# Final norm of an encoder with mixture of experts: who squares, scales and finishes each of the four tiles

## The chip, the cores and the metric

The kernel runs on one core of a Trainium2 chip. The metric is the device time of one execution in microseconds. A core has a matrix engine (TensorE, PE in the profile), three engines for elementwise work (VectorE or DVE, ScalarE or ACT, GpSimd or POOL) and SyncE (SP), whose queue issues most transfers. Each engine runs its own instructions in order, and engines wait for each other through semaphores.

## The reference

One layer of a bidirectional encoder on 512 tokens with 1024 channels: RMSNorm, a mixer (neighbourhood attention and gated linear attention), RMSNorm, a mixture of 32 experts (each token takes two), and a final RMSNorm. Cut to the end, on which the change works:

```python
def rmsnorm(x, g):
    xf = x.astype(jnp.float32)
    y = xf * lax.rsqrt(jnp.mean(xf * xf, axis=-1, keepdims=True) + RMS_EPS)
    return (y * g.astype(jnp.float32)).astype(x.dtype)

# in reference():
        h = rmsnorm(x, norm_ffn_g[l])
        x = x + hierarchical_moe(h, ...)      # x is x2 in the kernel
    return rmsnorm(x, final_norm_g)           # x2 * 1/root * gain, float32
```

## The kernel before, in words

The 512 tokens are four tiles of 128 rows (`TT = 4`, numbered 0 to 3), one row on each partition, 1024 columns (`D`) in float32. For most of the kernel TensorE multiplies by the experts' weights while SyncE loads them. The order of everything is written out by hand, one program for each engine.

The end is a pipeline over the four tiles:

- SyncE reads the stored expert outputs of each tile into `got`. TensorE adds up the rest of a tile (residual and the last expert) in two banks of PSUM, one for each half of 512 columns, and signals `share_done`.
- VectorE, in `add_up(t)`, adds `got` and the bank into `x2[:, t]`, half by half; each half counts `x2_done` up by one. So `x2_done` is 2 after tile 0, 8 after tile 3. Tile 1 is the one that `MIXED` names: two VectorE operations ahead of all tiles prepare it.
- ScalarE squares the tile with a running sum (`ssq3`; in the profile an ACTIVATE and an ACTIVATION_READ_ACCUMULATOR) and takes the root (`root3`).
- VectorE, in `final_root(t)`, takes the reciprocal of the root (`rstd3`).
- GpSimd multiplies tiles 0 to 2 by the gain `gfb` into `x2g`, one instruction a tile.
- ScalarE scales `x2g` by `rstd3` into `res` for tiles 0 to 2 (the Identity of line 1637); each is issued behind the root of the next tile.
- VectorE, in `last_tile()`, finishes tile 3 itself: one SCALAR_TENSOR_TENSOR for each half computes `x2 * rstd3 * gfb` (line 2255).
- SyncE waits for each result in the order of the tiles and stores it: three transfers of 512 KB (line 765), then two of 256 KB (line 769). Then it waits until all have landed, and the program ends.

A branch for tokens that overflow an expert's slots (`general > limit`) stands in the program and is not taken in these runs.

Of the kernel before, what the change touches and what calls it, by code (L numbers as in the profile page):

```python
# [224 lines left out]
def mixer_and_moe(nc, x, x_T, rpb, w_in, w_g2, b_g, gla_g, g_mix, w_out, g_ffn_T, w_r, b_r, w_all, g_fin,  # L225
                  c_small, c_mask, c_scan, c_tok, out, limit=SLOTS):
    with ExitStack() as ctx:
# [87 lines left out]
        def take(n):  # L315
            v = small[:, pos[0]:pos[0] + n]
            pos[0] += n
            return v
# [11 lines left out]
        ssq3, root3, rstd3 = take(TT), take(TT), take(TT)  # L330
        comb = take(2 * TT).rearrange("p (t k) -> p t k", k=2)
        most = take(1).bitcast(I32)
        eps = take(1)
        assert pos[0] <= 768

# [247 lines left out]
        def _(sp):  # L583
# [176 lines left out]
                    sp.dma_start(flat(down_unit(LAST)), down_d(e)).then_inc(a_w, 16)  # L760


            for t in range(TT - 1):
                sp.wait_ge(res_act, t + 1)
                sp.dma_start(out_d[t], res[:, t]).then_inc(out_stored, 16)
            for half in range(2):
                cols = slice(half * 512, (half + 1) * 512)
                sp.wait_ge(res_done, half + 1)
                sp.dma_start(out_d[TT - 1][:, cols], res[:, TT - 1, cols]).then_inc(out_stored, 16)
            sp.wait_ge(out_stored, 16 * (TT + 1))  # L770
            sp.wait_ge(page_cleared, 16)
            for t in range(TT):
# [635 lines left out]
        def _(act):  # L1408
# [217 lines left out]
                        nc.scalar.copy(g_hidT.rearrange("p a b -> p (a b)"), pbank[3][:]).then_inc(a_copied, 1)  # L1626

            nc.scalar.activation(oroot[:, 0, 0:1], oss[:, 0, 0:1], ACT.Sqrt)
            for t in range(TT):
                act.wait_ge(x2_done, 2 * (t + 1))  # L1630
                nc.scalar.activation(junk3[:, t], x2[:, t], ACT.Square, accum_out=ssq3[:, t:t + 1]).then_inc(sumsq_done, 1)
                act.wait_ge(sumsq_done, 3 * TT + t + 1)
                nc.scalar.activation(root3[:, t:t + 1], ssq3[:, t:t + 1], ACT.Sqrt, scale=1.0 / D, bias=eps).then_inc(root_done, 1)
                if t >= 1:
                    act.wait_ge(rstd_done, 2 * TT + t)
                    act.wait_ge(x2g_done, t)
                    nc.scalar.activation(res[:, t - 1], x2g[:, t - 1], ACT.Identity, scale=rstd3[:, t - 1:t]).then_inc(res_act, 1)


        @block.vector  # L1640
        def _(dve):
# [602 lines left out]
            def final_root(t):  # L2244
                dve.wait_ge(root_done, 2 * TT + t + 1)
                nc.vector.reciprocal(rstd3[:, t:t + 1], root3[:, t:t + 1]).then_inc(rstd_done, 1)

            def last_tile():
                t = TT - 1
                dve.wait_ge(x2_done, 2 * TT)  # L2250
                final_root(t)
                dve.wait_ge(rstd_done, 3 * TT)
                for half in range(2):
                    cols = slice(half * 512, (half + 1) * 512)
                    nc.vector.scalar_tensor_tensor(res[:, t, cols], x2[:, t, cols], rstd3[:, t:t + 1], gfb[:, cols], ALU.mult,
                                                   ALU.mult).then_inc(res_done, 1)

            dve.wait_ge(gf_in, 16)
            dve.wait_ge(most_done, 1)
# [1 line left out]
            with dve.If(general > limit):  # L2261
# [29 lines left out]
                dve.wait_ge(x2_done, 2 * TT)  # L2291
                nc.vector.memset(g_col, 0.0).then_inc(mix_step, 2)
                dve.wait_ge(mix_step, 2)
                for t in range(TT - 1):
                    final_root(t)
                last_tile()
            with dve.If(general < limit + 1):

                def add_up(t):
                    dve.wait_ge(pages_in[t], 32)  # L2300
                    for half in range(2):
                        cols = slice(half * 512, (half + 1) * 512)
                        dve.wait_ge(share_done, 2 * t + half + 1)
                        rest_of_it = pbank[SHARE_BANK[2 * t + half]][:]
                        if t == MIXED:
                            tt(x2[:, t, cols], got[0][:, t, cols], rest_of_it, ALU.add).then_inc(x2_done, 1)
                        else:
                            nc.vector.scalar_tensor_tensor(x2[:, t, cols], got[0][:, t, cols], comb_by[:, t, 0:1], rest_of_it,
                                                           ALU.mult, ALU.add).then_inc(x2_done, 1)

                dve.wait_ge(pages_in[MIXED], 32)
                nc.vector.tensor_scalar(got[1][:, MIXED], got[1][:, MIXED], comb_by[:, MIXED, 1:2], None,
                                        ALU.mult).then_inc(mix_step, 1)
                dve.wait_ge(mix_step, 1)
                nc.vector.scalar_tensor_tensor(got[0][:, MIXED], got[0][:, MIXED], comb_by[:, MIXED, 0:1], got[1][:, MIXED],
                                               ALU.mult, ALU.add).then_inc(mix_step, 1)
                add_up(0)
                dve.wait_ge(mix_step, 2)
                add_up(1)
                final_root(0)  # L2320
                add_up(2)
                final_root(1)
                add_up(3)
                final_root(2)
                last_tile()


        @block.gpsimd
        def _(pool):
# [33 lines left out]
                nc.gpsimd.indirect_dma_start(y_tok, bass.IndirectOffsetOnAxis(ap=tab_u[:, e:e + 1], axis=0), y_sb[e % RING], None,  # L2363
                                             bounds_check=last_row, oob_is_err=False).then_inc(y_stored[e % RING], 16)
            pool.wait_ge(gf_in, 16)
            for t in range(TT - 1):
                pool.wait_ge(x2_done, 2 * (t + 1))
                nc.gpsimd.tensor_tensor(x2g[:, t], x2[:, t], gfb, ALU.mult).then_inc(x2g_done, 1)


def constants():
# [73 lines left out]
```

## Time and profile before

| what | value |
|---|---|
| time, median of 3 runs | 736.91 us (736.15 to 736.98) |
| profiled execution, its own time | 737.39 us |
| span of its instructions | 735.6 us |
| PE busy | 718.7 us (98%) |
| DVE busy | 271.4 us (37%) |
| ACT busy | 146.6 us (20%) |
| POOL busy | 76.3 us (10%) |
| share of PE in the chain that ended last | 90% |
| mean DMA rate over the span | 327 GB/s |

The profiled execution lies 0.48 us over the median; its span leaves 1.8 us outside the first and the last instruction. TensorE is busy for nearly all of the span, but not in the last 8 us of it, and that is where the changed lines run. Shares over the whole span say nothing of that stretch, so it has to be read row by row.

### The profile page before, as it was taken

How to read it: one execution, taken by the hardware profiler on the slowest of the kernel's cores; microseconds unless marked ns; L12 is line 12 of the kernel's file. 1: busy time of each engine (PE TensorE's matmuls, PEld its weight loads, DVE VectorE, ACT ScalarE, POOL GpSimd, SP SyncE). 2: the span in 40 equal slices, each digit the busy share in tenths (PEclk: the TensorE clock that was granted, in tenths of full speed). 3: DMA queues.
4: the chain of work that ended last, by engine and by line, in shares of the span. 5: the costliest groups of instructions: out<-in, count | busy, mean ns of one | idle time of the engine just before them, and what ended most of it. 6: DMA issues, size and time to landing. Idle time of an engine off the chain costs nothing.

```text
span 735.6 us, 11813 instructions
## 1 busy us (share of the span) xinstructions
PE 718.7 (98%) x5112; PEld 411.6 (56%) x5117; DVE 271.4 (37%) x552; ACT 146.6 (20%) x315; POOL 76.3 (10%) x79
## 2 busy tenths in 40 slices
PE   9999999999999999999999999999999999998995
PEld 5488888888776664545544544544445445444431
DVE  2884463757987783111111111111111201201205
ACT  2652230134553550000000000000000000000014
POOL 0000049100000210010000010010010010000003
PEclk9999999999999999999999999999999999999998
DMA  9832332224934799999999999999999999999985
GB/s 326 265 114 93 142 112 73 99 67 158 412 118 174 269 355 380 425 430 424 397 421 429 439 429 437 432 419 438 429 419 429 434 421 428 427 424 428 423 344 210
DMA packets 31877, 240.79 MB, mean 327 GB/s; under 512 B 5606, under 2 KB 7014, under 8 KB 21456
## 3 DMA queue, kind: packets, MB, share of 16 engines
q1 hardware_dynamic: 29200, 235.94, 78.3%
q0 software_dynamic: 2480, 4.06, 1.5%
q8 instruction: 42, 0.69, 0.4%
q14 instruction: 11, 0.09, 0.0%
q10 hardware_dynamic: 144, 0.00, 0.0%
HBM read 231.74 MB, written 12.32 MB: 332 GB/s over the span
## 4 chain that ended last, share of the span: by engine, by line
PE 90%; DMA 7%; ACT 1%; DVE 1%; issue 0%; another core or an unknown queue 0%; DVEq 0%
PE bank L1272 27%; PE bank L785 17%; PE bank L1292 14%; PE bank L1213 9%; DMA arena<-in_w_all 7%; PE bank L829 4%; PE bank L1050 4%; PE bank L1106 3%; PE bank L1226 2%; PE bank L1281 1%; PE bank L1002 1%; PE bank L1088 1%; PE bank L1069 1%; PE bank L1147 1%; PE bank L1325 1%; PE bank L979 1%
## 5 line engine op out<-in xcount | busy, mean ns | idle before, releaser
L1272 PE MATMUL bank<-arena 128*64 128x512 f32 x1024 | 226.9, 593 | 3.9 <-DMA arena<-in_w_all 3.8
L1272 PEld LDWEIGHTS bank<-arena 128*64 128x64 f32 x1024 | 73.6, 137 | 148.8 <-issue 148.4
L785 PE MATMUL bank<-arena 128*128 128x256 f32 x560 | 123.2, 380 | 0.0
L1292 PE MATMUL bank<-arena 128*64 128x512 f32 x512 | 116.9, 598 | 0.2
L785 PEld LDWEIGHTS bank<-arena 128*128 128x128 f32 x560 | 105.7, 190 | 15.5 <-issue 1.5
L1643 DVE TENSOR_TENSOR arena<-arena 128x512 f32<-128x512 f32 (+12 forms) x129 | 96.0, 784 | 9.3 <-ACT arena L1411 6.1
L2188 DVE SCALAR_TENSOR_TENSOR arena<-bank,arena 128x256 f32<-128x256 f32 x32 | 15.5, 484 | 217.2 <-ACT arena L1597 217.1
L1213 PEld LDWEIGHTS bank<-arena 128*128 128x128 bf16 x1344 | 75.3, 98 | 22.2 <-issue 21.9
L1597 ACT ACTIVATE arena<-bank,arena 128x256 f32<-128x256 f32 x32 | 15.2, 475 | 339.9 <-PE bank L1272 334.1
L1213 PE MATMUL bank<-arena 128*128 128x128 bf16 (+1 forms) x1344 | 81.6, 217 | 0.0
L2363 POOL DMA_INDIRECT y_tok<-arena x31 | 30.3, 976 | 406.2 <-DVE arena L2195 378.4
L1292 PEld LDWEIGHTS bank<-arena 128*64 128x64 f32 x512 | 34.1, 136 | 58.4 <-issue 54.8
L2195 DVE COPY arena<-bank 128x512 f32<-128x512 f32 x32 | 22.1, 692 | 117.8 <-PE bank L1292 117.8
L1643 DVE TENSOR_TENSOR arena<-bank,arena 128x512 f32<-128x512 f32 (+1 forms) x49 | 32.6, 667 | 61.8 <-PE bank L1213 23.5
L829 PE MATMUL bank<-arena 128*128 128x512 f32 x64 | 28.8, 606 | 0.4 <-DVE arena L1650 0.4
L1411 ACT ACTIVATE arena<-bank 128x512 f32<-128x512 f32 x20 | 11.9, 596 | 81.7 <-PE bank L785 81.7
L1050 PE MATMUL bank<-arena 128*128 128x256 f32 x112 | 27.8, 391 | 0.0
L1106 PE MATMUL bank<-arena 128*128 128x512 f32 x56 | 25.3, 597 | 0.0
L1602 ACT COPY arena<-bank 128x256 f32<-128x256 f32 x32 | 11.9, 373 | 62.1 <-PE bank L1281 62.1
L1643 DVE TENSOR_TENSOR arena<-arena,bank 128x512 f32<-128x512 f32 (+1 forms) x31 | 20.6, 669 | 7.0 <-PE bank L1106 4.5
L1050 PEld LDWEIGHTS bank<-arena 128*128 128x128 f32 x112 | 20.1, 189 | 5.2 <-issue 2.7
L2356 POOL TENSOR_TENSOR arena<-arena 128x512 bf16<-128x512 f32 x8 | 8.3, 1042 | 127.6 <-DVE arena L1643 127.6
(179 smaller groups left out, 482.6 us busy)
## 6 DMA issues: line engine op xcount, KB each, us to landing
arena<-in_w_all SPq DMA_DIRECT2D x47, 2048.0 KB, 31.3
arena<-in_w_all SPq DMA_DIRECT2D x7, 6144.0 KB, 28.2
arena<-in_w_all SPq DMA_DIRECT2D x8, 4096.0 KB, 30.0
arena<-in_w_all SPq DMA_DIRECT2D x18, 1024.0 KB, 10.6
arena<-in_w_in SPq DMA_DIRECT2D x5, 2048.0 KB, 8.5
arena<-in_w_all SPq DMA_DIRECT2D x11, 512.0 KB, 5.2
arena<-in_x SPq DMA_DIRECT2D x8, 512.0 KB, 6.5
arena<-in_w_out SPq DMA_DIRECT2D x4, 1024.0 KB, 14.2
```

The source lines that it names most:

```text
L785: mm = pe.matmul(pbank[product_bank(g, p)][:, tile * 256:(tile + 1) * 256], lhs, rhs, start=(p in (1, 2, 5) and tile == 0 and k == 0), sto ...
L829: mm = pe.matmul(pbank[2 + t][:], gx[:, k, t * P:(t + 1) * P], w_buf[0][:, k], start=(k == 0), stop=(k == KC - 1))
L1050: mm = pe.matmul(pbank[share_bank(h, p)][:, tile * 256:(tile + 1) * 256], a[:, k, tile * P:(tile + 1) * P], w[:, k], start=(p in (1, 2, 5) ...
L1106: mm = pe.matmul(pbank[near_bank(m, p)][:], a[:, k], w[:, k], start=(p in (1, 2, 5) and k == 0), stop=(k == 1), skip_group_check=p in (6, ...
L1213: mm = pe.matmul(pbank[ROW_BANK[half]][:, k * P:k * P + n], h2_part[t][i][:, KC // 2 * half + k], pick[:, t, 0:n], start=(t == 0 and k == ...
L1272: mm = pe.matmul(both, xT[:, k, rows], gate_and_up(e, k)[:, :, cols], start=(k == 0), stop=(k == KC - 1))
L1292: mm = pe.matmul(pbank[down_bank(e)][64 * half:64 * half + 64, :], hidT[:, kc % 2, kc // 2], down_unit(e)[:, kc, half * 512:(half + 1) * 512],
L1597: nc.scalar.activation(hid[e % RING], pbank[GATE_BANK][:, 0:256], ACT.Silu, scale=rstd_slot[:, e:e + 1]).then_inc(sil_done, 1)
L1643: return nc.vector.tensor_tensor(out_, a, b, op)
L2188: nc.vector.scalar_tensor_tensor(hid[e % RING], pbank[GATE_BANK][:, 256:512], rstd_slot[:, e:e + 1], hid[e % RING], ALU.mult, ALU.mult).th ...
L2195: nc.vector.tensor_copy(y_sb[e % RING], pbank[down_bank(e)][:]).then_inc(y_evicted, 1)
L2363: nc.gpsimd.indirect_dma_start(y_tok, bass.IndirectOffsetOnAxis(ap=tab_u[:, e:e + 1], axis=0), y_sb[e % RING], None, bounds_check=last_row ...
```

## The change: the last RMSNorm is dealt out anew

Tile by tile:

- Tile 0: GpSimd multiplies only the first half by the gain, ScalarE scales that half; VectorE computes the second half in one SCALAR_TENSOR_TENSOR (`gained(0, 1)`), placed between the reciprocal of tile 0 and `add_up(2)`.
- Tile 1: GpSimd multiplies by the gain as before, and then scales the tile by `rstd3` too (a `tensor_scalar` on 1024 columns). ScalarE has no part in it but square and root. VectorE's reciprocal of tile 1 moves between the two halves of `add_up(2)`.
- Tile 2: VectorE computes both halves (`gained(2, 0)`, `gained(2, 1)`). GpSimd and ScalarE's Identity drop out.
- Tile 3: ScalarE squares the two halves in two instructions, each as soon as its half of `x2` is there. VectorE turns the first sum into a bias (`ms_half = ssq / D + eps`, one instruction on one column), and ScalarE's root adds it to the second sum. GpSimd multiplies the second half by the gain and ScalarE scales it, VectorE computes the first half.
- SyncE waits for the new semaphores and stores in the same order and the same sizes.

```diff
--- before.py
+++ after.py
@@ -330,6 +330,7 @@
         ssq3, root3, rstd3 = take(TT), take(TT), take(TT)
         comb = take(2 * TT).rearrange("p (t k) -> p t k", k=2)
         most = take(1).bitcast(I32)
+        ssq_half, ms_half = ssq2[:, 0, 0:1], ssq2[:, 0, 1:2]
         eps = take(1)
         assert pos[0] <= 768
 
@@ -760,13 +761,17 @@
                     sp.dma_start(flat(down_unit(LAST)), down_d(e)).then_inc(a_w, 16)
 
 
-            for t in range(TT - 1):
-                sp.wait_ge(res_act, t + 1)
-                sp.dma_start(out_d[t], res[:, t]).then_inc(out_stored, 16)
-            for half in range(2):
-                cols = slice(half * 512, (half + 1) * 512)
-                sp.wait_ge(res_done, half + 1)
-                sp.dma_start(out_d[TT - 1][:, cols], res[:, TT - 1, cols]).then_inc(out_stored, 16)
+            sp.wait_ge(res_act, 1)
+            sp.wait_ge(res_done, 1)
+            sp.dma_start(out_d[0], res[:, 0]).then_inc(out_stored, 16)
+            sp.wait_ge(x2g_done, 3)
+            sp.dma_start(out_d[1], res[:, 1]).then_inc(out_stored, 16)
+            sp.wait_ge(res_done, 3)
+            sp.dma_start(out_d[2], res[:, 2]).then_inc(out_stored, 16)
+            sp.wait_ge(res_done, 4)
+            sp.dma_start(out_d[TT - 1][:, 0:512], res[:, TT - 1, 0:512]).then_inc(out_stored, 16)
+            sp.wait_ge(res_act, 2)
+            sp.dma_start(out_d[TT - 1][:, 512:D], res[:, TT - 1, 512:D]).then_inc(out_stored, 16)
             sp.wait_ge(out_stored, 16 * (TT + 1))
             sp.wait_ge(page_cleared, 16)
             for t in range(TT):
@@ -1626,15 +1631,26 @@
                         nc.scalar.copy(g_hidT.rearrange("p a b -> p (a b)"), pbank[3][:]).then_inc(a_copied, 1)
 
             nc.scalar.activation(oroot[:, 0, 0:1], oss[:, 0, 0:1], ACT.Sqrt)
-            for t in range(TT):
+            for t in range(TT - 1):
                 act.wait_ge(x2_done, 2 * (t + 1))
                 nc.scalar.activation(junk3[:, t], x2[:, t], ACT.Square, accum_out=ssq3[:, t:t + 1]).then_inc(sumsq_done, 1)
                 act.wait_ge(sumsq_done, 3 * TT + t + 1)
                 nc.scalar.activation(root3[:, t:t + 1], ssq3[:, t:t + 1], ACT.Sqrt, scale=1.0 / D, bias=eps).then_inc(root_done, 1)
-                if t >= 1:
-                    act.wait_ge(rstd_done, 2 * TT + t)
-                    act.wait_ge(x2g_done, t)
-                    nc.scalar.activation(res[:, t - 1], x2g[:, t - 1], ACT.Identity, scale=rstd3[:, t - 1:t]).then_inc(res_act, 1)
+                if t == 1:
+                    act.wait_ge(rstd_done, 2 * TT + 1)
+                    act.wait_ge(x2g_done, 1)
+                    nc.scalar.activation(res[:, 0, 0:512], x2g[:, 0, 0:512], ACT.Identity, scale=rstd3[:, 0:1]).then_inc(res_act, 1)
+            t = TT - 1
+            act.wait_ge(x2_done, 2 * TT - 1)
+            nc.scalar.activation(junk3[:, t, 0:512], x2[:, t, 0:512], ACT.Square, accum_out=ssq3[:, t:]).then_inc(sumsq_done, 1)
+            act.wait_ge(x2_done, 2 * TT)
+            nc.scalar.activation(junk3[:, t, 512:D], x2[:, t, 512:D], ACT.Square, accum_out=ssq_half).then_inc(sumsq_done, 1)
+            act.wait_ge(sumsq_done, 4 * TT + 1)
+            act.wait_ge(mix_step, 3)
+            nc.scalar.activation(root3[:, t:], ssq_half, ACT.Sqrt, scale=1.0 / D, bias=ms_half).then_inc(root_done, 1)
+            act.wait_ge(rstd_done, 3 * TT)
+            act.wait_ge(x2g_done, 4)
+            nc.scalar.activation(res[:, t, 512:D], x2g[:, t, 512:D], ACT.Identity, scale=rstd3[:, t:]).then_inc(res_act, 1)
 
 
         @block.vector
@@ -2245,15 +2261,28 @@
                 dve.wait_ge(root_done, 2 * TT + t + 1)
                 nc.vector.reciprocal(rstd3[:, t:t + 1], root3[:, t:t + 1]).then_inc(rstd_done, 1)
 
-            def last_tile():
-                t = TT - 1
+            def gained(t, half):
+                cols = slice(half * 512, (half + 1) * 512)
+                nc.vector.scalar_tensor_tensor(res[:, t, cols], x2[:, t, cols], rstd3[:, t:t + 1], gfb[:, cols], ALU.mult,
+                                               ALU.mult).then_inc(res_done, 1)
+
+            def first_tile():
+                final_root(0)
+                dve.wait_ge(rstd_done, 2 * TT + 1)
+                gained(0, 1)
+
+            def last_tiles():
+
+                dve.wait_ge(sumsq_done, 4 * TT)
+                nc.vector.tensor_scalar(ms_half, ssq3[:, TT - 1:], 1.0 / D, EPS, ALU.mult, ALU.add).then_inc(mix_step, 1)
+                final_root(2)
                 dve.wait_ge(x2_done, 2 * TT)
-                final_root(t)
+                dve.wait_ge(rstd_done, 3 * TT - 1)
+                gained(2, 0)
+                gained(2, 1)
+                final_root(3)
                 dve.wait_ge(rstd_done, 3 * TT)
-                for half in range(2):
-                    cols = slice(half * 512, (half + 1) * 512)
-                    nc.vector.scalar_tensor_tensor(res[:, t, cols], x2[:, t, cols], rstd3[:, t:t + 1], gfb[:, cols], ALU.mult,
-                                                   ALU.mult).then_inc(res_done, 1)
+                gained(3, 0)
 
             dve.wait_ge(gf_in, 16)
             dve.wait_ge(most_done, 1)
@@ -2291,14 +2320,16 @@
...
             with dve.If(general < limit + 1):
 
                 def add_up(t):
                     dve.wait_ge(pages_in[t], 32)
                     for half in range(2):
+                        if (t, half) == (2, 1):
+                            final_root(1)
                         cols = slice(half * 512, (half + 1) * 512)
                         dve.wait_ge(share_done, 2 * t + half + 1)
                         rest_of_it = pbank[SHARE_BANK[2 * t + half]][:]
@@ -2317,12 +2348,10 @@
                 add_up(0)
                 dve.wait_ge(mix_step, 2)
                 add_up(1)
-                final_root(0)
+                first_tile()
                 add_up(2)
-                final_root(1)
                 add_up(3)
-                final_root(2)
-                last_tile()
+                last_tiles()
 
 
         @block.gpsimd
@@ -2363,9 +2392,15 @@
                 nc.gpsimd.indirect_dma_start(y_tok, bass.IndirectOffsetOnAxis(ap=tab_u[:, e:e + 1], axis=0), y_sb[e % RING], None,
                                              bounds_check=last_row, oob_is_err=False).then_inc(y_stored[e % RING], 16)
             pool.wait_ge(gf_in, 16)
-            for t in range(TT - 1):
-                pool.wait_ge(x2_done, 2 * (t + 1))
-                nc.gpsimd.tensor_tensor(x2g[:, t], x2[:, t], gfb, ALU.mult).then_inc(x2g_done, 1)
+            pool.wait_ge(x2_done, 2)
+            nc.gpsimd.tensor_tensor(x2g[:, 0, 0:512], x2[:, 0, 0:512], gfb[:, 0:512], ALU.mult).then_inc(x2g_done, 1)
+            pool.wait_ge(x2_done, 4)
+            nc.gpsimd.tensor_tensor(x2g[:, 1], x2[:, 1], gfb, ALU.mult).then_inc(x2g_done, 1)
+            pool.wait_ge(x2g_done, 2)
+            pool.wait_ge(rstd_done, 2 * TT + 2)
+            nc.gpsimd.tensor_scalar(res[:, 1], x2g[:, 1], rstd3[:, 1:2], None, ALU.mult).then_inc(x2g_done, 1)
+            pool.wait_ge(x2_done, 2 * TT)
+            nc.gpsimd.tensor_tensor(x2g[:, TT - 1, 512:D], x2[:, TT - 1, 512:D], gfb[:, 512:D], ALU.mult).then_inc(x2g_done, 1)
 
 
 def constants():
```

What stands in the engines' programs, as rows of line, operation, output and input, and semaphores waited for (`arena` is SBUF, `bank` PSUM). VectorE behind the last half of `add_up(1)`, before: the reciprocals of tiles 0, 1 and 2 stand between whole tiles.

```order
L1643 TENSOR_TENSOR arena<-arena,bank 128x512 [waits share_done]
L2246 RECIPROCAL arena<-arena 128x1 [waits root_done]
L2308 SCALAR_TENSOR_TENSOR arena<-arena,bank 128x512 [waits share_done,pages_in2]
L2308 SCALAR_TENSOR_TENSOR arena<-arena,bank 128x512 [waits share_done]
L2246 RECIPROCAL arena<-arena 128x1 [waits root_done]
L2308 SCALAR_TENSOR_TENSOR arena<-arena,bank 128x512 [waits share_done,pages_in3]
L2308 SCALAR_TENSOR_TENSOR arena<-arena,bank 128x512 [waits share_done]
```

The same place of the changed kernel (line 2266 is `gained`, 2262 the reciprocal, 2339 `add_up`):

```order
L1659 TENSOR_TENSOR arena<-arena,bank 128x512 [waits share_done]
L2262 RECIPROCAL arena<-arena 128x1 [waits root_done]
L2266 SCALAR_TENSOR_TENSOR arena<-arena 128x512 [waits rstd_done]
L2339 SCALAR_TENSOR_TENSOR arena<-arena,bank 128x512 [waits share_done,pages_in2]
L2262 RECIPROCAL arena<-arena 128x1 [waits root_done]
L2339 SCALAR_TENSOR_TENSOR arena<-arena,bank 128x512 [waits share_done]
L2339 SCALAR_TENSOR_TENSOR arena<-arena,bank 128x512 [waits share_done,pages_in3]
L2339 SCALAR_TENSOR_TENSOR arena<-arena,bank 128x512 [waits share_done]
```

An operation with both inputs in `arena` now stands ahead of `add_up(2)`; those of `add_up` have one input in `arena` and one in a bank. Behind them, at the end of VectorE's program, the changed kernel has these rows, where the one before had two reciprocals and two SCALAR_TENSOR_TENSOR:

```order
L2277 TENSOR_SCALAR arena<-arena 128x1 [waits sumsq_done]
L2262 RECIPROCAL arena<-arena 128x1 [waits root_done]
L2266 SCALAR_TENSOR_TENSOR arena<-arena 128x512 [waits rstd_done,x2_done]
L2266 SCALAR_TENSOR_TENSOR arena<-arena 128x512
L2262 RECIPROCAL arena<-arena 128x1 [waits root_done]
L2266 SCALAR_TENSOR_TENSOR arena<-arena 128x512 [waits rstd_done]
```

The reciprocal of tile 2 and both halves of tile 2 now stand behind the operation on tile 3's first sum. GpSimd's program ended in three multiplications of 1024 columns; in the changed kernel it ends so (line 2401 is the scaling of tile 1):

```order
L2392 DMA y_tok<-arena 2048x512 [waits y_evicted] x30
L2396 TENSOR_TENSOR arena<-arena 128x512 [waits x2_done,gf_in]
L2398 TENSOR_TENSOR arena<-arena 128x1024 [waits x2_done]
L2401 TENSOR_SCALAR arena<-arena 128x1024 [waits rstd_done,x2g_done]
L2403 TENSOR_TENSOR arena<-arena 128x512 [waits x2_done]
```

## Rows read from the trace of the kernel before

**Rows 1.** The page: the chain that ended last, by engine.

```profile
PE 90%; DMA 7%; ACT 1%; DVE 1%; issue 0%; another core or an unknown queue 0%; DVEq 0%
```

**Rows 2.** The chain that ended last, in order of time: start, us, what.

```profile
727.48 1.13 ACT arena L1637
728.61 1.05 ACT arena L1631 x2
...
730.08 0.17 DVE arena L2246
...
730.28 0.75 DVE arena L2255
```

**Rows 3.** Timeline of VectorE, the end: start, us, operation, count, idle before.

```profile
721.96 1.28 DVE L1643 TENSOR_TENSOR arena<-arena,bank 128x512 f32<-128x512 f32 x2
723.59 0.17 DVE L2246 RECIPROCAL arena<-arena 128x1 f32<-128x1 f32 x1 [0.35 <-ACT arena L1633]
724.65 1.41 DVE L2308 SCALAR_TENSOR_TENSOR arena<-arena,bank 128x512 f32<-128x512 f32 x2 [0.90 <-PE bank L1334]
725.97 0.16 DVE L2246 RECIPROCAL arena<-arena 128x1 f32<-128x1 f32 x1
726.57 1.54 DVE L2308 SCALAR_TENSOR_TENSOR arena<-arena,bank 128x512 f32<-128x512 f32 x2 [0.44 <-PE bank L1325]
```

**Rows 4.** Timeline of ScalarE, the end.

```profile
723.04 0.19 ACT L1631 ACTIVATION_READ_ACCUMULATOR arena<-arena 128x1 f32 x1
723.26 0.30 ACT L1633 ACTIVATE arena<-arena 128x1 f32<-128x1 f32 x1
723.46 1.04 ACT L1631 ACTIVATE arena<-arena 128x1024 f32<-128x1024 f32 x1
...
729.88 1.14 ACT L1637 ACTIVATE arena<-arena 128x1024 f32<-128x1024 f32 x1
```

**Rows 5.** Timelines of GpSimd and SyncE, the end; line 769 by itself.

```profile
722.20 7.02 POOL L2368 TENSOR_TENSOR arena<-arena 128x1024 f32<-128x1024 f32 x3 [18.23 <-DVE arena L2308]
...
731.04 0.33 SPq L765 DMA_DIRECT2D out<-arena  x1
...
731.42 0.43 SPq L769 DMA_DIRECT2D out<-arena  x1
...
L769 SPq DMA_DIRECT2D out<-arena x2: 431/610/789, 731.4 to 731.9; - x2
...
DMA to landing us min/median/max: 3.2/3.2/3.3
```

**Rows 6.** Busy time by stretches of 0.4 us; last: clock, DMA share, GB/s.

```profile
731.80:732.20 0.40, 0.00 (x0) 0.00 (x0) 0.00 (x0) 0.00 (x0) 0.00 (x0) 0.50 0.85 348
...
734.60:735.00 0.40, 0.00 (x0) 0.00 (x0) 0.00 (x0) 0.00 (x0) 0.00 (x0) 0.50 0.05 15
```

**Rows 7.** Timelines of GpSimd and VectorE where they overlapped; line 2340 by itself.

```profile
107.96 1.22 DVE L1643 TENSOR_TENSOR arena<-arena 128x1024 f32<-128x1024 f32 x1
...
L2340 POOL COPY arena<-arena x8: 1056/1078/2141, 102.9 to 111.1; 128x512 f32<-128x512 f32 x8
...
261.94 1.10 DVE L1643 TENSOR_TENSOR arena<-arena 128x128 bf16<-128x128 f32 x1
261.85 1.04 POOL L2356 TENSOR_TENSOR arena<-arena 128x512 bf16<-128x512 f32 x1 [0.96 <-DVE arena L1643]
...
267.24 0.28 DVE L2042 SCALAR_TENSOR_TENSOR arena<-arena 128x1 f32<-128x1 f32 x1 [0.45 <-ACT arena L1532]
266.46 1.04 POOL L2356 TENSOR_TENSOR arena<-arena 128x512 bf16<-128x512 f32 x1 [3.57 <-DVE arena L1643]
```

**Rows 8.** Timeline of ScalarE at 243.5 us: a square of 512 columns.

```profile
243.50 0.63 ACT L1532 ACTIVATE arena<-arena 128x512 f32<-128x512 f32 x1
244.03 0.19 ACT L1532 ACTIVATION_READ_ACCUMULATOR arena<-arena 128x1 f32 x1
244.13 0.60 ACT L1553 COPY arena<-arena 128x512 bf16<-128x512 bf16 x1
```

More of the change, by code:

```diff
@@ L2293, in _ @@
                 dve.wait_ge(mix_step, 2)
-                for t in range(TT - 1):
-                    final_root(t)
-                last_tile()
+                first_tile()
+                final_root(1)
+                last_tiles()
             with dve.If(general < limit + 1):
@@ L2301, in add_up @@
                     for half in range(2):
+                        if (t, half) == (2, 1):
+                            final_root(1)
                         cols = slice(half * 512, (half + 1) * 512)
@@ L2319, in _ @@
                 add_up(1)
-                final_root(0)
+                first_tile()
                 add_up(2)
-                final_root(1)
                 add_up(3)
-                final_root(2)
-                last_tile()
+                last_tiles()
         @block.gpsimd
@@ L2365, in _ @@
             pool.wait_ge(gf_in, 16)
-            for t in range(TT - 1):
-                pool.wait_ge(x2_done, 2 * (t + 1))
-                nc.gpsimd.tensor_tensor(x2g[:, t], x2[:, t], gfb, ALU.mult).then_inc(x2g_done, 1)
+            pool.wait_ge(x2_done, 2)
[7 more added lines that the diff above has]
+            nc.gpsimd.tensor_tensor(x2g[:, TT - 1, 512:D], x2[:, TT - 1, 512:D], gfb[:, 512:D], ALU.mult).then_inc(x2g_done, 1)
 def constants():
```

## The prediction, made before the change was run

> **What bounds the kernel now.** I read the page first: the chain that ended last is 90% TensorE [rows 1], but the changed lines all run behind 722 us, and VectorE waits for TensorE there for the last time at 726.57 [rows 3]. So the question is only what sets the end of the last 14 us. The chain in order of time gives it: ScalarE scales tile 1 at 727.48, squares tile 3 at 728.61, VectorE takes the reciprocal at 730.08 and computes the first half of tile 3 at 730.28 [rows 2]. ScalarE is the tight engine here: VectorE has finished tile 3's `x2` at 726.57 + 1.54 = 728.11 [rows 3], and the square starts only when ScalarE is through with tile 1, so tile 3 loses 0.5 us there.
>
> Behind the last computation lies the output. SyncE issues tile 2 at 731.04 (released by the Identity that ends at 729.88 + 1.14 = 731.02 [rows 4]), then the halves of tile 3 at 731.42 and 731.9 [rows 5]. These three hold 512 + 256 + 256 KB. The DMA engines move at full rate from 731.8, and nothing is left from 734.6 on [rows 6]: 1 MB in one burst of 2.8 us, which starts 0.8 us behind the issue of tile 2. The last half was issued at 731.9 and alone would need some 0.7 us of transfer behind the same 0.8 us, so it would be moved by 733.4; it ended at 734.6 because it queued. **The end of the kernel therefore follows the issue of tile 2, not that of tile 3**, as long as the halves of tile 3 are issued less than about 1.2 us later than now relative to it. All sums below are for this moment, 731.04.
>
> **What VectorE and GpSimd do to each other.** The change gives VectorE operations with both inputs in SBUF (`gained` reads `x2` and `gfb`) while GpSimd works. In the stage as it is no such pair meets: `add_up` has one input in a bank, and line 2255 runs when GpSimd is done (722.20 + 7.02 = 729.22 [rows 5]). Elsewhere it does. A VectorE operation of 128 columns that began at 261.94, just behind a GpSimd one (261.85 + 1.04 = 262.89), took 1.10 us, nearly as long as the 1.22 us of one with 1024 columns, and ended at 263.04. A SCALAR_TENSOR_TENSOR of one column began at 267.24 and took 0.28 us, until 267.52, where a GpSimd operation ended at 267.50; a reciprocal of one column takes 0.17 [rows 3]. The other way about, VectorE's operation at 107.96 took its plain 1.22 us, and of GpSimd's eight copies around it one took 2.14 us against a median of 1.08 [rows 7]. So the later of the two is held until the earlier is done, and a held VectorE operation ends at GpSimd's end plus its streaming time: 0.15 us for 128 columns, so about 0.55 for 512 (an estimate from the last two figures of rows 3 and 7: 0.75 us for a whole operation less the 0.15 to 0.2 that one column takes). A price of nothing for this meeting is the other bound.
>
> The Trainium skill says the same in the page "SBUF — State Buffer" (section Who interferes with whom): the second to issue fully blocks until the first is done. It speaks against this change, and the trace agrees with it at 261.94 (1.10 us for 128 columns). By the rule the sum is the +0.6 us below, without it the −1.0 us.
>
> **The change, part by part, with the hold.**
> 1. `gained(0, 1)`. The reciprocal of tile 0 is done at 723.76 [rows 3]; the operation would run from 723.8 to 724.55 and fit ahead of `add_up(2)`, which waits for TensorE until 724.65. But GpSimd's half of tile 0 takes about 1.19 us (7.02 / 3 = 2.34 for 1024 columns [rows 5], half of it and a little), 722.20 to 723.39, and tile 1's `x2` is there at 721.96 + 1.28 = 723.24. So GpSimd starts tile 1 at 723.40 and reads until 725.75. `gained(0, 1)` is held and ends at 725.75 + 0.55 = 726.30 instead of 724.55.
> 2. Queued behind it on VectorE: `add_up(2)`, the reciprocal of tile 1, `add_up(3)`. TensorE's shares are all there by 726.57 plus one half, so they go through back to back at a pitch of 0.66 (1.41 for two of 0.75) and 0.08 for the reciprocal: the first half from 726.21, reciprocal until 727.04, second half until 727.70 (before: 726.06), tile 3 until 728.36 and 729.03 (before: 728.11). Tile 2's `x2` is 1.6 us late, tile 3's 0.9 us.
> 3. ScalarE. Of three Identities of 1.14 us there remain a half of tile 0 and a half of tile 3. That frees it, so it waits for VectorE now. Square of tile 2 from 727.73, its its sum read 0.96 later (a square lasts 1.06, and the read begins 0.10 before its end [rows 8]), root 0.22 behind that at 728.91 until 729.21 (as 723.04 to 723.26 [rows 4]). The first half of tile 3 is squared 0.20 later, 729.11 (as 723.26 to 723.46), sum read at +0.53, done 729.83; the second half starts 0.10 behind that read's start [rows 8], 729.74, its sum is read at 730.27, root 730.49 to 730.79. Before, this root ended at 730.0: the halves do not pay back the 0.9 us.
> 4. The new wait. VectorE's `ms_half` needs the first sum, 729.83, and runs 729.87 to 730.02 (as a reciprocal). The reciprocal of tile 2 and both `gained(2, ...)` stand behind it, though tile 2's root was there at 729.21. Reciprocal until 730.11, then `gained(2, 0)` at 730.15.
> 5. GpSimd. The scaling of tile 1 waits for the reciprocal of 727.04 and starts at 727.08. No row shows a `tensor_scalar` on GpSimd. From below, I take half of the nearest row's rate, 1.05, since any value under 2.05 gives one result; by the nearest row, GpSimd's copies of 512 columns at 1.06 each, 1024 take 2.1; from above, the two-input 2.37. I take 2.1, the copy being the nearest in kind: until 729.2. Then tile 3's half, 729.2 to 730.4. `gained(2, 0)` meets it: 730.40 + 0.55 = 730.95 instead of 730.90. This hold costs 0.05 us, and 0.3 with 2.37; with anything under 2.05 nothing.
> 6. Tile 2's second half ends at 731.61, and SyncE issues tile 2 at 731.63 against 731.04: **+0.6 us**. Tile 3: reciprocal until 731.68, `gained(3, 0)` until 732.46, ScalarE's half (0.71: 0.63 for a square of that size plus the 0.08 between 1.14 and 1.06) until 732.4; issues at 732.49 and 732.93. That is 0.86 and 1.30 us behind tile 2's; before, 0.38 and 0.86. The burst from 732.4 lasts 2.8 us, the last half is ready for it at 733.7, so it still queues. Tiles 0 and 1 are issued at 726.3 and 729.2 and have left the DMA engines before 732.4.
>
> The GPSIMD page of the Trainium skill ("GPSIMD Engine Reference", section Performance versus the Vector engine) has one-input bodies at 1.03 cycles per element; no run here shows it for this operation. By it the scaling would take about 1 us, an estimate from that page, and the sum would be +0.55.
>
> **Sum.** Removed: 1.14 us twice from ScalarE ahead of tile 3. Added: a hold of 1.75 us on VectorE of which 1.6 reaches tile 2. Net at the issue of tile 2: +0.6 us. Against the profiled execution: span 735.6 to 736.2, time 737.39 to 738.0. The median of the runs shown lies 0.48 us lower, so 736.91 + 0.6 = 737.5 us.
>
> **The rivals.**
> - *No hold* (a SCALAR_TENSOR_TENSOR of this size gets through, or VectorE is there first). For it: margin between 723.40 and 723.80 is only 0.4 us. Against it: rows 7. Then `add_up(2)` ends at 726.19, square of tile 2 at 726.22, root until 727.70; tile 3's first half squared 727.60, second 728.23, root until 729.28; first sum 728.32, `gained(2, ...)` 728.64 to 730.05, issue of tile 2 at 730.07: −1.0 us, tile 3 at 730.93 and 731.35. Time 735.9.
> - *The end follows tile 3's issue instead.* If the last half needs its 3.2 us to land from 732.93, against 731.9 before [rows 5], the price is +1.0: 737.9.
> - *GpSimd's scaling is slow*, the case on the other side. Its place is between 727.08 and the last GpSimd half, and every us beyond 2.05 goes through `gained(2, 0)` to the issue of tile 2: the loss is its duration less 1.54. It becomes measurable from 3.0 us on; at 4.2, twice the copy's price, the loss is 2.7 us and the time 739.6. For it: the operation takes a scale from memory for each partition, which no GpSimd row has. Against it: the GpSimd rows here lie at 2.0 (1.04 for 512 columns [rows 7]) to 2.3 ns a column, and 3.0 would be needed.
> - *It doesn't do what it says*: the Identity of tile 1 left ScalarE for nothing if `x2` is late anyway; that is part 3 of the forecast.
>
> **How the numbers follow.** Hold and end by tile 2: 0.60, time 737.5, own range 737.2 to 737.8. End by tile 3: 0.10. No hold: 0.20. Slow scaling: 0.10. A measurement of this kernel tells a change from none at about 0.2%, 1.5 us. Neither +0.6, +1.0 nor −1.0 reaches that; what can is the slow scaling (0.10, and a little for two prices together) and the no-hold case with scatter in its favour (runs spread 0.8 us). Faster 0.06, same 0.82, slower 0.12. The range takes in no hold and the end by tile 3 with some scatter: 736.0 to 738.3.
>
> **What would show it.** Right: one SCALAR_TENSOR_TENSOR of 512 columns of about 2.5 us starting near 723.8 on VectorE; TensorE no longer the releaser of `add_up(2)`; the square of tile 2 near 727.7; a GpSimd `tensor_scalar` near 2.1 us; tile 2 issued near 731.6. Wrong: that operation at 0.75 us, the square of tile 2 at 726.2, tile 2 issued at 730.1; or a scaling over 3 us. The weakest steps are the streaming time of a held operation, the unseen `tensor_scalar`, and that the burst begins 0.8 us behind tile 2's issue.

## The result, and the profile after

The changed kernel is slower: the ratio of its time to that of the kernel before is 1.0026, 95% interval 1.0014 to 1.0038, which is 1.9 us (1.0 to 2.8). The medians over 22 runs each are 737.99 us and 735.89 us. The span of the profiled execution is 734.5 us, shorter than before. That tells nothing of the change: in this trace the last stage begins 2.45 us earlier (the first `add_up` operation starts at 718.19, against 720.64 before). In every trace here the stage is compared from that operation on; I call the time from there to the end of the span **the stretch**. Before it is 735.6 − 720.64 = 14.96 us, after it is 734.5 − 718.19 = 16.31 us: 1.35 us more. Two rows of VectorE's timeline before are needed for this section, the first `add_up` operations and the two of tile 3:

```profile
720.64 1.40 DVE L2308 SCALAR_TENSOR_TENSOR arena<-arena,bank 128x512 f32<-128x512 f32 x2
...
730.28 1.41 DVE L2255 SCALAR_TENSOR_TENSOR arena<-arena 128x512 f32<-128x512 f32 x2
```

The changed kernel's timeline, VectorE and then GpSimd (start, us, operation, count, idle before); rows of before are [rows 3] and [rows 5]:

```profile
718.19 1.40 DVE L2339 SCALAR_TENSOR_TENSOR arena<-arena,bank 128x512 f32<-128x512 f32 x2
...
721.33 2.56 DVE L2266 SCALAR_TENSOR_TENSOR arena<-arena 128x512 f32<-128x512 f32 x1
723.81 0.73 DVE L2339 SCALAR_TENSOR_TENSOR arena<-arena,bank 128x512 f32<-128x512 f32 x1
...
724.54 2.04 DVE L2339 SCALAR_TENSOR_TENSOR arena<-arena,bank 128x512 f32<-128x512 f32 x3
727.42 0.15 DVE L2277 TENSOR_SCALAR arena<-arena 128x1 f32<-128x1 f32 x1 [0.84 <-ACT arena L1645]
...
727.75 2.35 DVE L2266 SCALAR_TENSOR_TENSOR arena<-arena 128x512 f32<-128x512 f32 x2
```

```profile
719.75 1.27 POOL L2396 TENSOR_TENSOR arena<-arena 128x512 f32<-128x512 f32 x1 [18.27 <-DVE arena L2339]
720.98 2.35 POOL L2398 TENSOR_TENSOR arena<-arena 128x1024 f32<-128x1024 f32 x1
724.80 2.85 POOL L2401 TENSOR_SCALAR arena<-arena 128x1024 f32<-128x1024 f32 x1 [1.47 <-DVE arena L2262]
727.63 1.25 POOL L2403 TENSOR_TENSOR arena<-arena 128x512 f32<-128x512 f32 x1
```

Put the two lists side by side. VectorE's `gained(0, 1)` starts at 721.33, 0.35 us after GpSimd's multiplication of tile 1 has started. It lasts 2.56 us and ends at 723.89, 0.56 us behind that multiplication's end (723.33). The pair for tile 2 starts at 727.75, 0.12 us after the start of GpSimd's last operation, and takes 2.35 us, where line 2255 took 1.41 for two before (0.75 for one [rows 2]). `add_up`, with one input in a bank, keeps its pitch under GpSimd's scaling (2.04 for three), as it did under GpSimd's multiplications before (1.41 for two [rows 3, 5]).

ScalarE and SyncE of the changed kernel:

```profile
725.30 1.06 ACT L1636 ACTIVATE arena<-arena 128x1024 f32<-128x1024 f32 x1 [2.22 <-DVE arena L2339]
...
728.03 0.29 ACT L1650 ACTIVATE arena<-arena 128x1 f32<-128x1 f32 x1
730.20 0.72 ACT L1653 ACTIVATE arena<-arena 128x512 f32<-128x512 f32 x1 [1.88 <-DVE arena L2262]
```

```profile
730.12 0.33 SPq L770 DMA_DIRECT2D out<-arena  x1
730.98 0.33 SPq L772 DMA_DIRECT2D out<-arena  x1
731.36 0.45 SPq L774 DMA_DIRECT2D out<-arena  x1
```

ScalarE waits 2.22 us for tile 2 and 1.88 us for the reciprocal of tile 3, while before it had no gap over 0.12 us between 722.08 and 731.02. Tile 2 is issued at 730.12, 11.93 us behind the first `add_up` operation; before it was 731.04 − 720.64 = 10.40 [rows 5]. That is 1.53 us later, and the stretch is 1.35 us longer. The busy time by stretches (TensorE, its weight loads, VectorE, ScalarE, GpSimd; the last three are clock, DMA share, GB/s) shows the burst of 1 MB once more:

```profile
730.40:730.80 0.40, 0.00 (x0) 0.00 (x0) 0.40 (x1) 0.40 (x1) 0.00 (x0) 0.50 0.00 0
730.80:731.20 0.40, 0.00 (x0) 0.00 (x0) 0.16 (x1) 0.12 (x1) 0.00 (x0) 0.50 0.66 266
...
733.60:734.00 0.40, 0.00 (x0) 0.00 (x0) 0.00 (x0) 0.00 (x0) 0.00 (x0) 0.50 0.11 36
```

It begins some 0.8 us behind tile 2's issue and lasts 2.7 to 2.8 us, as in [rows 6].

### The profile page after: what moved, and what is told of

Same layout as the page of the kernel before. It is cut to its first block, busy times and chain, and to the rows that moved or that the text cites. A ratio compares the mean times of both kernels' runs of the same rounds, so it can differ in the third digit from the quotient of the medians.

```text
span 734.5 us, 11820 instructions
## 1 busy us (share of the span) xinstructions
PE 717.8 (98%) x5112; PEld 411.2 (56%) x5117; DVE 275.7 (38%) x555; ACT 144.7 (20%) x316; POOL 77.0 (10%) x80
## 4 chain that ended last, share of the span: by engine, by line
PE 85%; DMA 10%; ACT 2%; DVE 2%; issue 1%; SPq 1%; DVEq 0%; POOLq 0%
PE bank L1277 26%; PE bank L790 17%; PE bank L1297 14%; PE bank L1218 9%; DMA arena<-in_w_all 7%; PE bank L1055 4%; PE bank L1111 3%; PE bank L834 2%; PE bank L1231 2%; DMA arena<-in_x 1%; PE bank L1007 1%; PE bank L1286 1%; PE bank L1093 1%; DMA arena<-y_tok 1%; PE bank L1074 1%; DMA y_tok<-arena 1%
```

## The experiments

The theory: VectorE's operations with two SBUF inputs are held by GpSimd's two-input operations, and what this makes late is tile 2. The rivals: these operations are slow by themselves; the loss is GpSimd's slow scaling alone; the end follows tile 3. The stretch comes from one trace of one execution each; two traces of the same kernel differ by up to 0.3 us (the last section of experiments). The timed ratios, with intervals of about ±0.15% (1.1 us), carry less.

| kernel | `gained(0, 1)`, us | square of tile 2 starts at | tile 2 issued at | stretch | ratio to before (95%) |
|---|---|---|---|---|---|
| before | none | 5.45 | 10.40 | 14.96; again 14.71 | 1 |
| changed | 2.56 | 7.11 | 11.93 | 16.31; again 16.34 | 1.0026 (1.0014 to 1.0038) |
| 1 GpSimd waits | 0.75 | 5.50 | 9.76 | 15.04 | 1.0003 (0.9986 to 1.0020) |
| 2 VectorE ends tile 3 | 2.55 | 7.10 | 10.99 | 15.37 | 1.0002 (0.9988 to 1.0016) |
| 3 gain in PSUM | 0.75 | 5.89 | 9.75 | 14.38 | 0.9999 (0.9983 to 1.0014) |
| 4 ScalarE scales tile 1 | 2.55 | 7.52 | 11.39 | 15.76 | 1.0007 (0.9995 to 1.0019) |
| 5 = 1 and 2 | 0.75 | 5.50 | 9.77 | 15.10 | 1.0001 (0.9988 to 1.0015) |
| 6 tile 2 ahead of the sum | 2.55 | 7.10 | 11.33 | 15.69 | 1.0028 (1.0012 to 1.0044) |
| 7 no overlap | 0.75 | 5.45 | 9.45 | 14.78; again 13.94 | 0.9992 (0.9979 to 1.0004); 1.0005 (0.9988 to 1.0021) |
| 8 before, half of tile 0 alone | 2.54 | 7.03 | 11.98 | 16.37 | 1.0031 (1.0019 to 1.0042) |

Positions count from the start of the first `add_up` operation of the same trace.

### 1. GpSimd waits for VectorE's half of tile 0

```diff
             pool.wait_ge(x2_done, 4)
+            pool.wait_ge(res_done, 1)
             nc.gpsimd.tensor_tensor(x2g[:, 1], x2[:, 1], gfb, ALU.mult).then_inc(x2g_done, 1)
```

Expected: 

> GpSimd's multiplication of tile 1 waits until VectorE has written the second half of tile 0; all else as in the changed kernel. The measure is the stretch from the start of the first add_up operation to the end of the span: 14.95 us in the kernel before, 16.3 in the changed one. Hold theory (the later of the two engines is held by the other's reads): VectorE's operation on tile 0 falls from 2.56 to 0.75 us, the square of tile 2 starts 5.6 us behind the first add_up operation instead of 7.1, and since GpSimd's scaling (2.85 us) now ends about 1.2 us behind the point where VectorE wants to start tile 2, a new hold of 1 to 1.7 us appears there: stretch 14.9 to 16.0. Rival, the operation is slow by itself (a first use, or its two inputs): it stays at 2.5 us, and the stretch grows to 17.5, since GpSimd starts later.

Timeline of this kernel, VectorE and GpSimd:

```profile
722.10 0.75 DVE L2266 SCALAR_TENSOR_TENSOR arena<-arena 128x512 f32<-128x512 f32 x1
...
726.91 1.41 DVE L2266 SCALAR_TENSOR_TENSOR arena<-arena 128x512 f32<-128x512 f32 x2
...
728.43 1.66 DVE L2266 SCALAR_TENSOR_TENSOR arena<-arena 128x512 f32<-128x512 f32 x1
...
722.99 2.37 POOL L2399 TENSOR_TENSOR arena<-arena 128x1024 f32<-128x1024 f32 x1 [1.21 <-DVE arena L2266]
725.46 2.85 POOL L2402 TENSOR_SCALAR arena<-arena 128x1024 f32<-128x1024 f32 x1
728.29 1.25 POOL L2404 TENSOR_TENSOR arena<-arena 128x512 f32<-128x512 f32 x1
```

The operation takes 0.75 us: it was held, it is not slow by itself. But the new hold that I expected at tile 2 did not come. The pair at 726.91 runs at its plain 1.41 us while GpSimd's one-input scaling goes on until 728.31; the operation at 728.43 is held by the two-input one, 1.66 us, until 0.55 us behind its end at 729.54. Tile 2 is issued 2.2 us earlier than in the changed kernel, yet the stretch gives back only 1.3: see experiment 5. The timed ratio falls from 1.0026 to 1.0003.

### 2. VectorE ends tile 3

GpSimd's last multiplication and ScalarE's last scaling are taken out, SyncE waits for VectorE instead, and:

```diff
                 gained(3, 0)
+                gained(3, 1)
```

Expected: 

> VectorE computes both halves of tile 3; GpSimd's last multiplication and ScalarE's last scaling are gone. Hold theory: the first hold stays (2.56 us), the second goes, since GpSimd is through with its scaling about 9.5 us behind the first add_up operation, when VectorE is ready for tile 2: the two operations on tile 2 take 1.41 us instead of 2.35, tile 2 is issued 1.0 us earlier, the stretch falls from 16.3 to 15.5 although VectorE now has one operation more behind it. Rival, the end follows tile 3: the added operation (0.66 us) cancels most of it, 16.0 or more.

```profile
729.08 1.42 DVE L2263 SCALAR_TENSOR_TENSOR arena<-arena 128x512 f32<-128x512 f32 x2
```

The pair for tile 2 (VectorE's timeline above) is back from 2.35 to 1.42 us, tile 2 is issued at 10.99, and the stretch is 15.37. So the second hold cost 0.94 us. Tile 2 now goes out where the prediction had put it for the changed kernel (731.63 − 720.64 = 10.99), since the second hold was the part that it had made too small.

### 3. The gain in PSUM

ScalarE copies the gain into tile 0's two banks once they are free, and VectorE reads it there:

```diff
-                nc.vector.scalar_tensor_tensor(res[:, t, cols], x2[:, t, cols], rstd3[:, t:t + 1], gfb[:, cols], ALU.mult,
+                nc.vector.scalar_tensor_tensor(res[:, t, cols], x2[:, t, cols], rstd3[:, t:t + 1], pbank[SHARE_BANK[half]][:], ALU.mult,
```

Expected: 

> ScalarE copies the gain into the two banks of tile 0 once they are free (two copies of 0.6 us), and VectorE reads it from there, so that each of its operations has one input in SBUF; GpSimd's work is unchanged. Hold theory: no VectorE operation of 512 columns takes over 0.8 us any more, though GpSimd works at the same times; tile 2 is issued about 9.7 us behind the first add_up operation, the stretch is 14.2 to 14.5, under the 14.95 of the kernel before. Rival, the operations are slow for another reason than the second SBUF input: they stay at 2.5 and 1.6 us and the stretch at 16.3 or more.

Timeline, VectorE and GpSimd:

```profile
724.04 0.75 DVE L2270 SCALAR_TENSOR_TENSOR arena<-arena,bank 128x512 f32<-128x512 f32 x1
...
728.63 1.41 DVE L2270 SCALAR_TENSOR_TENSOR arena<-arena,bank 128x512 f32<-128x512 f32 x2
...
723.12 2.35 POOL L2404 TENSOR_TENSOR arena<-arena 128x1024 f32<-128x1024 f32 x1
...
728.52 1.26 POOL L2409 TENSOR_TENSOR arena<-arena 128x512 f32<-128x512 f32 x1
```

This is the clearest of the tests. Both VectorE entries begin while a two-input GpSimd operation runs, as in the changed kernel, and neither is held. What VectorE does differs only in the place of one input; the first entry starts 0.6 us later than in the changed kernel, behind ScalarE's copy, but still 1.4 us ahead of GpSimd's end. The stretch is 14.38, though ScalarE has 1.2 us more to do.

### 4. ScalarE scales tile 1

```diff
+                if t == 2:
+                    act.wait_ge(rstd_done, 2 * TT + 2)
+                    act.wait_ge(x2g_done, 2)
+                    nc.scalar.activation(res[:, 1], x2g[:, 1], ACT.Identity, scale=rstd3[:, 1:2]).then_inc(res_act, 1)
                 act.wait_ge(x2_done, 2 * (t + 1))
```

GpSimd's `tensor_scalar` is taken out. Expected: 

> Tile 1 is scaled by ScalarE, ahead of the square of tile 2, and GpSimd's scaling of 2.85 us is gone. Hold theory: the first hold stays (2.56 us); the scaling of 1.14 us starts with tile 1's reciprocal and delays the square of tile 2 by 0.4 us; GpSimd's last multiplication ends before VectorE wants to start tile 2, so no second hold: stretch 15.9 against 16.3. Rival, GpSimd's scaling costs nothing and the added ScalarE work is on the path: 16.7.

Timeline, VectorE and GpSimd:

```profile
728.09 1.42 DVE L2270 SCALAR_TENSOR_TENSOR arena<-arena 128x512 f32<-128x512 f32 x2
...
726.61 1.26 POOL L2404 TENSOR_TENSOR arena<-arena 128x512 f32<-128x512 f32 x1 [3.33 <-DVE arena L2343]
```

GpSimd's last multiplication is over at 727.87, ahead of the pair for tile 2, and the pair takes 1.42 us instead of 2.35. Against that, ScalarE's scaling of tile 1 delays the square of tile 2 by 0.4 us. Tile 2 is issued at 11.39 and the stretch is 15.76, 0.55 us less than with GpSimd's scaling.

### 5. Both first edits

Expected: 

> The edits of the first two experiments together: GpSimd's multiplication of tile 1 waits for VectorE's half of tile 0, and VectorE computes both halves of tile 3. Stretch from the start of the first add_up operation to the end of the span. If the end follows the stored bytes (my theory: tiles 1, 2 and 3 leave in one burst of 1.5 MB, 4.2 us, that begins 0.8 us behind the issue of tile 1), it stays near the 15.0 us of the first experiment although tile 3's first half is issued 0.9 us earlier. Rival, the end follows the issue of tile 3's last half: 14.4 us.

SyncE's timeline:

```profile
729.18 0.34 SPq L768 DMA_DIRECT2D out<-arena  x1
729.57 0.43 SPq L770 DMA_DIRECT2D out<-arena  x1
730.05 0.78 SPq L772 DMA_DIRECT2D out<-arena  x1
730.87 1.20 SPq L774 DMA_DIRECT2D out<-arena  x1
```

and the busy time by stretches:

```profile
729.60:730.00 0.40, 0.00 (x0) 0.00 (x0) 0.40 (x2) 0.00 (x0) 0.00 (x0) 0.50 0.00 0
730.00:730.40 0.40, 0.00 (x0) 0.00 (x0) 0.40 (x2) 0.00 (x0) 0.00 (x0) 0.50 0.98 399
733.60:734.00 0.40, 0.00 (x0) 0.00 (x0) 0.00 (x0) 0.00 (x0) 0.00 (x0) 0.50 0.97 369
734.00:734.40 0.40, 0.00 (x0) 0.00 (x0) 0.00 (x0) 0.00 (x0) 0.00 (x0) 0.50 0.05 15
```

Tile 1, late because of GpSimd's 2.85 us, opens a burst of 1.5 MB that fills 730.0 to 734.0. The first half of tile 3 is issued 0.9 us earlier than in experiment 1 (10.25 against 11.16), and the stretch is the same, 15.10 against 15.04. The end follows the bytes still to be stored, not the last issue; by that rival it would have come at 14.4.

### 6. Tile 2 ahead of the sum

```diff
-                dve.wait_ge(sumsq_done, 4 * TT)
-                nc.vector.tensor_scalar(ms_half, ssq3[:, TT - 1:], 1.0 / D, EPS, ALU.mult, ALU.add).then_inc(mix_step, 1)
                 final_root(2)
                 dve.wait_ge(x2_done, 2 * TT)
                 dve.wait_ge(rstd_done, 3 * TT - 1)
                 gained(2, 0)
+                dve.wait_ge(sumsq_done, 4 * TT)
+                nc.vector.tensor_scalar(ms_half, ssq3[:, TT - 1:], 1.0 / D, EPS, ALU.mult, ALU.add).then_inc(mix_step, 1)
```

Expected: 

> The changed kernel, with the reciprocal and first half of tile 2 ahead of VectorE's operation on tile 3's first sum. The first experiment showed two VectorE operations at 1.41 us while GpSimd's one-input scaling ran. Theory A, a one-input GpSimd operation does not hold VectorE: the first half of tile 2 runs at 0.75 us under the scaling, only the second half is held by GpSimd's multiplication for tile 3; tile 2 is issued 0.6 us earlier than in the changed kernel, stretch 15.7 against 16.3. Theory B, any GpSimd operation that reads SBUF holds it: the first half is held until the scaling ends, 1.2 us or more, and the stretch stays at 16.3.

Timeline, VectorE and GpSimd:

```profile
729.29 0.75 DVE L2266 SCALAR_TENSOR_TENSOR arena<-arena 128x512 f32<-128x512 f32 x1
...
730.02 1.69 DVE L2266 SCALAR_TENSOR_TENSOR arena<-arena 128x512 f32<-128x512 f32 x1
...
727.02 2.85 POOL L2401 TENSOR_SCALAR arena<-arena 128x1024 f32<-128x1024 f32 x1 [1.46 <-DVE arena L2262]
729.84 1.32 POOL L2403 TENSOR_TENSOR arena<-arena 128x512 f32<-128x512 f32 x1
```

Theory A: 0.75 us under the scaling, 1.69 us under the multiplication. The order that I had named in the prediction costs 0.6 us of the stretch (16.31 to 15.69). The timed ratio, 1.0028, doesn't show that gain; its interval of ±0.16% doesn't exclude it either. Experiment 4 has nearly the same stretch (15.76) and a ratio of 1.0007. So the traces order the variants more finely than the timed runs can confirm: the kernel ahead of the stretch scatters by more than any of these differences (in the two traces of the changed kernel the first `add_up` operation starts at 718.19 and at 721.76).

### 7. No overlap, and once more

GpSimd waits as in 1, ScalarE scales tile 1 behind the root of tile 2, the first half of tile 2 stands ahead of the sum, and VectorE ends tile 3:

```diff
                 if t == 1:
...
+                if t == 2:
+                    act.wait_ge(rstd_done, 2 * TT + 2)
+                    act.wait_ge(x2g_done, 2)
+                    nc.scalar.activation(res[:, 1], x2g[:, 1], ACT.Identity, scale=rstd3[:, 1:2]).then_inc(res_act, 1)
```

Expected: 

> The version that the experiments point to: GpSimd's multiplication of tile 1 waits for VectorE's half of tile 0; ScalarE scales tile 1 behind the root of tile 2; tile 2 stands ahead of the sum on VectorE; VectorE computes both halves of tile 3; GpSimd has nothing to do behind tile 1. Theory: no VectorE operation is held; tile 1 is issued 8.1 us behind the first add_up operation, tile 2 8.9, tile 3 10.6 and 11.3; stretch 14.0 to 14.2 us, against 14.95 of the kernel before and 16.3 of the changed one; time 0.1% under the kernel before. Rival, the root of tile 3 now comes late behind ScalarE's scaling and sets the end: 14.7 or more.

Measured: none of VectorE's operations of 512 columns in this stage is over 0.76 us, but the stretch is 14.78, not 14.1. That is the number of the rival, in which the root of tile 3 sets the end. The busy time by stretches shows why:

```profile
732.80:733.20 0.40, 0.00 (x0) 0.00 (x0) 0.00 (x0) 0.00 (x0) 0.00 (x0) 0.50 0.79 302
733.20:733.60 0.40, 0.00 (x0) 0.00 (x0) 0.00 (x0) 0.00 (x0) 0.00 (x0) 0.50 0.06 20
733.60:734.00 0.40, 0.00 (x0) 0.00 (x0) 0.00 (x0) 0.00 (x0) 0.00 (x0) 0.50 0.07 26
```

The full rate ends at 733.2, 13.1 us behind the first operation, as the theory had it. Then 6 to 7% of the DMA engines' time, the share of one engine of 16, goes on for nearly 1 us: the trace has single packets of 0.08 us there, each beginning where the one before ends. Once more: 

> The version of the seventh experiment once more. There the full-rate stretch of the stores ended 13.1 us behind the first add_up operation, as expected, but a few packets at a low share went on for 0.9 us, and the stretch was 14.8 instead of 14.1. If that straggling is chance, the stretch comes out near 14.1 now, with tile 2 issued at 9.45 again and the root of tile 3 at 9.2. If it belongs to this version, it is 14.8 again. Time 0.1% under the kernel before.

```profile
731.20:731.60 0.40, 0.00 (x0) 0.00 (x0) 0.00 (x0) 0.00 (x0) 0.00 (x0) 0.50 0.88 338
731.60:732.00 0.40, 0.00 (x0) 0.00 (x0) 0.00 (x0) 0.00 (x0) 0.00 (x0) 0.50 0.02 5
```

No straggler, stretch 13.94, tile 2 issued at 9.46 again. The same program did both, so the straggler is chance, and the root of tile 3 is not what sets the end, since it starts at 9.2 in both traces. The late engine is not rare either: the traces of the kernel before (both) and of experiment 4 have one behind the burst of tile 1, where it is not at the end. The timed runs put this version at 0.9992 and 1.0005 of the kernel before, no difference that can be told. The 0.8 us by which its better trace is ahead (14.71 − 13.94) is 0.1% of the time, and its other trace shows no gain.

### 8. The half of tile 0 alone, on the kernel before

```diff
                 add_up(1)
-                final_root(0)
+                first_tile()
                 add_up(2)
```

Expected: 

> The kernel before with one part of the change: VectorE computes the second half of tile 0 between its reciprocal and add_up(2), GpSimd multiplies and ScalarE scales the first half only. Hold theory: that operation takes 2.56 us, the square of tile 2 starts 7.1 us behind the first add_up operation instead of 5.45, tile 2 is issued 1.6 us later, and the stretch grows from 14.95 to 16.5. Rival, the loss of the changed kernel is GpSimd's slow scaling alone: the stretch stays at 15.0 or falls, ScalarE being relieved by 0.5 us.

```profile
723.97 2.54 DVE L2253 SCALAR_TENSOR_TENSOR arena<-arena 128x512 f32<-128x512 f32 x1
```

2.54 us (VectorE's timeline), stretch 16.37, ratio 1.0031: this part by itself brings a loss as large as that of the whole change, with no GpSimd scaling in the program. The rival that put the loss on the scaling alone is out. It follows that the other parts of the change, the relief of ScalarE on one side and the second hold and the wait for `ms_half` on the other, come to about nothing together.

### 9 and 10. Before and changed once more

Expected: 

> The kernel before, unchanged, once more: how far does the stretch from the first add_up operation to the end of the span differ between two profiled executions? The issues of the five transfers should lie within 0.1 us of the first trace's; the landing of the last may differ by some tenths. If the stretch of 14.95 us comes out over 15.7 or under 14.2, the differences between the kernels are not told by one trace each.

Expected: 

> The changed kernel, unchanged, once more. Hold theory: 2.56 us for VectorE's half of tile 0 and 2.35 for tile 2 again, since their causes are fixed in the program; stretch 16.3 within 0.3. If the holds were chance, the durations would differ.

The stretches are 14.71 (14.96 the first time) and 16.34 (16.31); tile 2 issued at 10.33 and 11.93, the holds at 2.55 and 2.35 us. One trace tells the issues to 0.1 us, the landing of the last bytes to some 0.3, and 0.8 with a straggler.

## Why the prediction came out as it did

The prediction named the mechanism and the sign of the likeliest case; its size was too small. The forecast was +0.6 us, the measured one is +1.9 (1.0 to 2.8) by the runs and 1.35 to 1.6 by the traces (16.31 − 14.96, 16.34 − 14.71). I gave "no change that can be measured" 0.82, and the measured 0.26% lies just over the bound of 0.2% that I used; its interval reaches to both sides of it.

That the time itself fits, 737.5 us forecast and 737.99 measured, is in part luck. The kernel before has a median of 735.89 over 22 runs, 1.0 us less than the 736.91 of three runs that I added to. From 735.89 the same sum gives 736.5. The loss that I had too small, by 1.3 us and more, made up for a base that was 1.0 us too high.

- **Part 1, the first hold**: right. Forecast start 723.8 and end 726.30 on the clock of the first trace; measured, shifted by 2.45, 723.78 and 726.34. Experiments 1, 3 and 8 show it by taking it away and by making it alone.
- **Parts 2 and 3**: right to 0.05 us. `add_up` through at 729.03 (forecast 729.03), square of tile 2 at 727.75 (727.73), root of tile 3 at 730.48 (730.49).
- **Part 4, the new wait**: right in place, start of `ms_half` 729.87 as forecast; experiment 6 priced it at 0.6 us.
- **Part 5, GpSimd's scaling**: the term that was mis-sized. I took 2.1 us from the copy, with 2.37 as the upper bound; it lasts 2.85, and the last multiplication 1.25 instead of 1.2. The estimate of 1 us that stands beside them is further off still. With 0.18 us between the reciprocal and its start, where I had 0.04, GpSimd begins that multiplication at 730.08 and ends at 731.33, not 730.4. So the hold of tile 2 cost 0.94 us and not 0.05. The upper bound did not hold: this one-input operation with a scale from memory for each partition is dearer here than the two-input one (2.85 us against 2.35). Whether it is the scale that makes it dear was not tried. My rival of a slow scaling, to which I gave 0.10, had the mechanism and the formula; by its formula, 2.85 gives +1.3. So the loss is that of two cases together, the first hold and the slow scaling.
- **Part 6**: the burst begins 0.8 us behind tile 2's issue and the end follows it, +1.53 at the issue and +1.35 at the end. Experiment 5 shows the limit of that rule: when tile 1 is late as well, the burst starts with tile 1.

Of the rivals, *no hold* is excluded by the trace, and *the end follows tile 3's issue* by experiment 5. The Trainium skill's rule ("SBUF — State Buffer", Who interferes with whom) holds where both operations read two tensors: 2.56 us against 0.75. For GpSimd's one-input scaling the runs differ from it: VectorE's two-input operations ran at 0.75 us each, or 1.41 to 1.42 for two, beside it in experiments 1, 5 and 6, and the scaling kept its 2.85. All three start in its second half; whether it holds at its start was not tried.

## What to carry to other kernels

Before work is dealt to a second elementwise engine, list which operations of VectorE and GpSimd overlap and how many SBUF inputs each has: a 0.75 us operation slipped in for free was held until a GpSimd one was over, and everything behind it on VectorE went with it. Reading one input from PSUM removed the hold and left the work where it was, at the price of two copies on ScalarE (1.2 us) and of two banks that were free. At the end of a kernel count the bytes that are still to be stored, not the last issue: here 1 MB takes 2.8 us. An earlier start of that burst shortened the stretch (experiments 2 and 3), an earlier issue of the last stores did not (experiment 5).

## What the runs showed of the hardware that I had not expected

- GpSimd's `tensor_scalar` with a scale for each partition on 128x1024 float32 takes 2.85 us, its `tensor_tensor` 2.35.
- That scaling did not hold VectorE's two-input operations (0.75 and 1.41 us for one and two of 512 columns), while `tensor_tensor` held them until 0.55 us behind its own end.
- SyncE's issue of a store takes longer when others were issued just before: 0.34, 0.43, 0.78 and 1.20 us for four issued within 1.7 us (experiment 5), where a lone one takes 0.33 to 0.35.
- In one trace of two of the same program, a single DMA engine's leftover packets made the end 0.8 us later (experiment 7).
